# Two-map attention on one core: the value products of a pair of tiles in one run behind the next tile's scores, and three orders that go with it

## The reference, cut to what matters

```python
def diff_attention(q, k, v, pos, slopes, lam):
    # q, k: [B, L, H, 2, 64]; v: [B, L, H, 128]
    def block(qb, pb):
        s = jnp.einsum('bqhmd,bkhmd->bhmqk', qb, k) * scale
        s = s - slopes * dist
        p = jax.nn.softmax(s, axis=-1)
        w = p[:, :, 0] - lam * p[:, :, 1]
        return jnp.einsum('bhqk,bkhe->bqhe', w, v)
```

## Time and profile before

| | |
|---|---|
| median of 3 runs | 3316.82 us (3316.59 to 3317.58) |
| the profiled execution | 3318.04 us, of which span 3316.2 us |
| TensorE matmul busy | 3175.5 us (96%), 19990 instructions |
| TensorE weight loads busy | 2813.7 us (85%) |
| VectorE, ScalarE, GpSimd busy | 54%, 35%, 30% |
| the two-map attention | from about 1306 us of the span to about 1945 us |

### The profile page before, as it was taken

How to read it: one execution, slowest core, us unless ns; L and a number is a source line. 1 busy time by engine, 2 the same in 40 slices (tenths; PEclk the granted TensorE clock), 3 DMA queues, 4 the chain that set the end, 5 groups by cost and what they waited for, 6 DMA issues and landing times.

```text
span 3316.2 us, 51851 instructions
## 1 busy us (share of the span) xinstructions
PE 3175.5 (96%) x19990; PEld 2813.7 (85%) x19990; DVE 1799.1 (54%) x3108; ACT 1145.6 (35%) x2293; POOL 990.4 (30%) x688
## 2 busy tenths in 40 slices
PE   8999999999999999999999889999999999799997
PEld 6677768788888888888888789999999999799997
DVE  5554556755554545788888741277678033522223
ACT  3433333333322213555555541156466110300002
POOL 3112223787772333222221132210000222122222
PEclk9999999999999999999999999999999999899998
DMA  4011112122224112000000012211111341478888
GB/s 158 26 32 33 33 64 102 64 77 77 77 98 195 45 44 97 23 23 23 26 25 22 16 49 85 76 40 51 38 48 45 107 177 56 179 248 311 310 312 291
DMA packets 98390, 315.27 MB, mean 95 GB/s; under 512 B 15266, under 2 KB 31586, under 8 KB 95008
## 3 DMA queue, kind: packets, MB, share of 16 engines
q1 hardware_dynamic: 68448, 248.16, 21.2%
q10 hardware_dynamic: 23600, 45.98, 3.7%
q0 software_dynamic: 6160, 18.63, 2.2%
HBM read 249.55 MB, written 57.86 MB: 93 GB/s over the span
## 4 chain that ended last, share of the span: by engine, by line
PE 45%; DVE 7%; ACT 4%; issue 3%; DMA 1%; POOL 0%; ACTq 0%; SPq 0%; DVEq 0%; POOLq 0%
PE PS L683 14%; PE PS L3733 6%; PE PS L671 4%; PE PS L3480 4%; PE PS L3763 3%; ACT EA L2277 3%; PE PS L3514 3%; PE PS L3272 3%; PE PS L3241 3%; PE PS L3556 3%; PE PS L3316 2%; DVE EA L2754 1%; DVE EA L2738 1%; DVE PA_lo L2765 1%; DVE EB L2916 1%
## 5 line engine op out<-in xcount | busy, mean ns | idle before, releaser
L705 POOL CAST w_hi<-ring 128x1024 fp32r<-128x1024 f32 x130 | 137.8, 1060 | 1568.1 <-PE PS L683 390.4
L707 POOL TENSOR_TENSOR w_lo<-ring,w_hi 128x1024 fp32r<-128x1024 f32 x130 | 326.4, 2511 | 10.5
L2277 ACT ACTIVATE EA<-EA,small_sb 128x1040 f32<-128x1040 f32 x144 | 166.8, 1159 | 222.2 <-DVE small_sb L2738 222.2
L2738 DVE CUSTOM_DVE_ANT_0 EA<-PS,biasH,low_a 128x1024 f32<-128x1024 f32 x128 | 163.6, 1278 | 25.1 <-PE PS L3272 23.1
L3241 PE MATMUL PS<-u_hi,w_hi 128*128 128x348 f32 x504 | 171.1, 339 | 0.5
L3241 PE MATMUL PS<-u_lo,w_hi 128*128 128x348 f32 x504 | 162.2, 322 | 0.0
L3241 PE MATMUL PS<-u_hi,w_lo 128*128 128x348 f32 x504 | 162.0, 321 | 0.0
L1671 DVE TENSOR_TENSOR hid_lo<-hid,hid_hi 128x1024 fp32r<-128x1024 f32 x44 | 91.8, 2124 | 118.7 <-ACT hid_hi L1313 118.7
L1763 PE MATMUL PS<-u_hi,w_hi 128*128 128x512 f32 x352 | 146.9, 417 | 3.0 <-POOL w_lo L707 2.3
L1960 PE MATMUL PS<-t_hi,slot_hi 128*128 128x512 f32 x352 | 139.8, 397 | 5.9 <-DVE t_lo L1572 3.2
L1960 PE MATMUL PS<-t_hi,slot_lo 128*128 128x512 f32 x352 | 139.1, 395 | 0.0
(11 more groups left out here) (522 smaller groups left out, 9017.0 us busy)
## 6 DMA issues: line engine op xcount, KB each, us to landing
ring<-in_stream SPq DMA_DIRECT2D x130, 512.0 KB, 3.5
w_gate_sb<-in_w_gate SPq DMA_DIRECT2D x64, 512.0 KB, 6.9
w_up_sb<-in_w_up SPq DMA_DIRECT2D x64, 512.0 KB, 7.1
w_down_sb<-in_w_down SPq DMA_DIRECT2D x64, 512.0 KB, 5.6
gu_raw<-in_gate_up SPq DMA_DIRECT2D x22, 1024.0 KB, 5.5
hid_keep<-hid_out SPq DMA_DIRECT2D x17, 512.0 KB, 2.9
hid<-hid_keep ACTq DMA_DIRECT2D x15, 512.0 KB, 16.5
x_keep<-xT ACTq DMA_DIRECT2D x1, 4176.0 KB, 14.6
```

The costliest lines, as they stand in the source:

```text
L705: pool.tensor_copy(w_hi[j][:, :, :], w_raw[j][:, :, :]).then_inc(S["w_rounded"], 1)
L707: pool.tensor_tensor(w_lo[j][:, :, :], w_raw[j][:, :, :], w_hi[j][:, :, :], ALU.subtract).then_inc(S["w_split"], 1)
L2277: act.activation(e[0:m, :], e[0:m, :], ACT.Exp, scale=-1.0, bias=small[0:m, 8 + 2 * par + k:9 + 2 * par + k], accum_out=small[0:m, 12 + 2 ...
L2738: dve.tensor_tensor_reduce(e[0:m, 0:T1], wide(2 * k, T1, m), bias, -1.0, low_a[0:m, t, k:k + 1], ALU.add, ALU.min, low).then_inc(S["aa_max ...
```

## The change

`values` is no longer cut into halves. All 27 matmuls of a group stand where the second half stood, behind the scores of the even step; the first half's places at t = 1, 3, 5 and 8 are gone. The two waits for `probs_lo` stay, each ahead of its part. In ScalarE's list `take_columns` moves behind the `exp` of map 1. In the last head's even steps `turn_probs` moves ahead of `woven_gate`. Nothing is computed that was not, and the instructions are the same in number.

```diff
@@ ScalarE, head()
                         if after:
                             exp(after[0], (after[1] + after[2]) % 2, after[2], 0)
-                        if t % 2 == 0 and before:
-                            take_columns(*before)
                         if t % 2 or t == NT:
                             take_pt(h, t)
                         if after:
                             exp(after[0], (after[1] + after[2]) % 2, after[2], 1)
+                        if t % 2 == 0 and before:
+                            take_columns(*before)
                         if t % 2 == 0 and t < NT:
                             take_pt(h, t)
@@ TensorE
-                def values(h, g, half):
+                def values(h, g):
 
                     n, w = 9 * h + A_GROUPS[g][-1], group_width(g)
-                    pe.wait_ge(S["probs_lo"], 3 * n + 2 + half)
-                    if g == 0:
-                        pe.wait_ge(S["values_lo"], 3 * h + 2 + half)
-                    for i in (range(4, NT + 1) if half else range(4)):
+                    for i in range(NT + 1):
+                        if i % 4 == 0 and i < NT:
+                            pe.wait_ge(S["probs_lo"], 3 * n + 2 + i // 4)
+                            if g == 0:
+                                pe.wait_ge(S["values_lo"], 3 * h + 2 + i // 4)
...
-                    if half:
-                        last.then_inc(S["aa_o"], 1)
+                    last.then_inc(S["aa_o"], 1)
@@ TensorE, head()
                         if before:
-                            values(*before, 1)
+                            values(*before)
                         kind, c = UNITS[t]
                         unit(h + 1, 1 - odd, kind, c, 0)
                         turn_probs(h, (odd + t) % 2, t, first)
                         unit(h + 1, 1 - odd, kind, c, 1)
-                        if t in (1, 3, 5, NT):
-                            values(h, min(t // 2, NGA - 1), 0)
                         if before:
                             turn_back(*before, 9 * h + t)
@@ TensorE, the last head
                     if t % 2 == 0:
-                        values(*group_before(h, t), 1)
+                        values(*group_before(h, t))
+                        turn_probs(h, (1 + t) % 2, t, False, False)
                     if t == 0:
                         pe.wait_ge(S["aa_vf"], 3 * h + 3)
                     woven_gate(*WOVEN[t])
-                    turn_probs(h, (1 + t) % 2, t, False, False)
-                    if t in (1, 3, 5):
-                        values(h, t // 2, 0)
-                    if t % 2 == 0:
+                    if t % 2:
+                        turn_probs(h, (1 + t) % 2, t, False, False)
+                    else:
                         turn_back(*group_before(h, t), 9 * h + t)
@@ TensorE, the last head, drain()
-                        for half in range(2):
-                            values(h, NGA - 1, half)
+                        values(h, NGA - 1)
```

## The result

The changed kernel takes 3322.13 us in the median of 13 runs (3318.78 to 3325.03), the kernel before 3316.75 us beside it (13 runs, of which one took 7910 us and doesn't move the median). The ratio is 1.0016, with a 95% interval of 1.0009 to 1.0024: about 5 us slower. That is clear of the noise, but less than the 0.2% that I had called no change. The profiled execution takes 3321.27 us with a span of 3319.5, 3.3 us more than before.

A forecast was written before the change was run, and what follows sets the result against it. TensorE sets the pace of heads 0 to 6, VectorE close behind and pacing the last head. 7 x (0.63 + 0.60 - 1.31) + 6 x 0.35 - 0.3 = +1.3 us, so 3318 us, no change; range 3298 to 3325.

The forecast's parts named there:

- rival (a): Steps 3 and 6: columns not late, VectorE has slack; gains 1.09 and 1.31 us a head, 3299 us; chance 0.13.
- the pairs of steps: Steady heads: steps 1 and 2 take 17.2 us (before 16.58), 3 and 4 18.3 (17.70), 5 and 6 17.7 (19.01).
- T1: Start of step 1 on TensorE; VectorE's first pass over step 2's scores was put 9.84 us after it.
- T3: Start of step 3 on TensorE; VectorE's first pass over step 4's scores was put 10.94 us after it.
- Step 4's wait: Steady heads, step 4: transposes wait 1.7 us for the columns; steps 3 and 4 together +0.60 us a head.
- The wait of step 8: Step 8: not removed, 1.5 us at meta_scores; 1.60 us of products move into step 0; +0.35 us in heads 1 to 6.
- In step 6: Step 6: no wait ahead of turn_back; steps 5 and 6 together -1.31 us a head (bound -0.9).
- Rival (b): Step 3: VectorE's short copy slips ahead of GpSimd's L707; 1.15 us less in step 4, 3310 us; chance 0.14.
- +0.27: Steady heads: a head of 80.4 us against 80.17.
- rival (c): Heads: clock falls behind step 4's wait of 1.7 us; 12 us over 7 heads, 3330 us; chance 0.08.
- -0.3 us: Last head: -0.43 in steps 1, 3, 5; +0.1 in steps 2, 4; +0.8 in step 6; step 0 even.
- S + 4.16: TensorE's transposes can start 4.16 us after S, the start of VectorE's first pass over that step's scores.

The follow-up runs named there:

- V: Kernel before, only all value products of a group put behind the next tile's scores: 3306.18 us, ratio 0.9962.
- C: Kernel before, only take_columns put behind the second exponential: 3327.7 us, ratio 1.0032.
- G: Kernel before, only the last head's even steps turning tiles ahead of the gate's products: 3314.12 us, ratio 0.9994.
- the reduction: VectorE's 16-column copy of meta_a issued as a reduction over a length-1 axis: 3296.64 us in the changed kernel, 3299.14 us in the kernel before.

## Why the prediction was right, and where it wasn't

**Right, by its steps.** The sum of a gain and a loss near each other was the answer: V takes the waits ahead of the values away, C puts waits ahead of the transposes. What I had as rival (a), that the columns are not late, 3299 us, is what the kernel without C does (3300.6). The lengths of the pairs of steps came within 0.13 us of the forecast, each a little shorter, since I started VectorE's pass some 0.1 to 0.2 us late (it comes at T1 + 9.63 in step 2, forecast 9.84, and at T3 + 10.72 in step 4, forecast 10.94). Step 4's wait is 1.47 us instead of 1.7. The wait of step 8 stood up at the meta scores, as the order had shown. In step 6 there is none. Rival (b) stayed close: in step 3 the copy starts 0.09 us behind L707, where it was 0.23:

```profile
1572.78 2.40 POOL L707 TENSOR_TENSOR w_lo<-ring,w_hi 128x1024 fp32r<-128x1024 f32 x1
1572.87 2.34 DVE L2735 COPY EA<-meta_a 128x16 f32<-128x16 f32 x1
```

From step 1 of head 0 to step 1 of the last I had +1.5 us, and measured +1.9, but that they are so close is luck. The steps themselves didn't lengthen a head (80.2 us where the clock stays up, 80.1 to 80.5 before), where I had +0.27 for most. Three falls of the clock, 0.95 each, added 2.9 us that I hadn't priced, and head 0, head 2 and head 6 came out 0.3, 0.3 and 0.7 us shorter than before. Of the 5 us by which the kernel is slower, the forecast had 1.3.

**Wrong: the clock in the heads.** I priced a fall in step 4, behind the wait of 1.7 us, as rival (c), 0.08 and 12 us. It came in step 0 instead, behind the wait of 1.46 us at the meta scores, and in three heads alone. A wait of the same length at the same clock stood before in step 8 without a fall, with 12 value products behind it; the experiment that puts them back has no falls, and over all the traces the half clock follows the wait at the meta scores 13 times of 36, and the one ahead of value products never. I moved these products and kept the wait, but didn't ask what the clock would make of that.

**Wrong: the last head.** I had -0.3 us, from -0.43 for each odd step and little for the even ones. Steps 1 to 7 became 0.7 longer. The pairs of steps take 16.88, 16.95 and 17.65 us instead of 17.52, 17.27 and 15.96, where I expected about 17.2, 16.9 and 16.3. The first two fit by luck: before, they held one fall of the clock each, in the scores of steps 1 and 3, which I left in and which is gone; in its place the transposes of steps 2 and 4 run at half clock. The last pair had no fall before, and there the new one shows: in step 6 I had a gate piece of 12 matmuls, but not the half clock that it now runs at. That TensorE would stand 3.4 us in one piece followed from my own numbers (transposes at S + 4.16), and half a clock behind such a stretch was in sight in the earlier trace rows; I wrote that the clock could be worth 3 us either way and put nothing in the sum. That G makes this worse the text said in words (the gate "now stands behind it"), but priced at some tenths: by the ratios it is 4 to 6 us. Step 2 is 1.7 us longer than in the changed kernel without G (12.40 against 10.70). From its transposes to `turn_back` it has 3.63 us; the same work at full clock takes 2.41 in step 2 of the kernel with G alone, its wait taken off, and without G there are 1.90 us, a wait of 0.76 in them. So by this estimate the order is worth 0.5 us a step, near my tenths, and the half clock 1.2.

**Not foreseen: the tail.** From step 7 to the output projection takes 1.4 us more. Windows of about 9 us from the first transposes of the finished heads, the kernel before and then the changed one:

```profile
1954.00:1963.00 9.00, 6.66 (x37) 6.42 (x38) 4.29 (x6) 2.23 (x2) 3.81 (x3) 0.81 0.42 163
1963.00:1972.00 9.00, 9.00 (x70) 8.93 (x69) 4.71 (x5) 4.47 (x4) 8.48 (x6) 1.00 0.12 30
```

```profile
1956.00:1965.00 9.00, 5.49 (x38) 5.21 (x39) 4.50 (x5) 2.24 (x2) 4.25 (x3) 0.97 0.40 156
1965.00:1974.00 9.00, 9.00 (x59) 8.95 (x58) 4.16 (x4) 3.45 (x4) 6.97 (x5) 0.84 0.17 48
```

The clock is low once in each, for about the same time. Before, it is low ahead of a wait for `oa_lo`, which hides it; after, the wait comes first (3.52 us instead of 2.13) and the low clock falls on 59 matmuls, where there were 70. All kernels with any of the three parts have some of it, 1.3 to 3.3 us; the two with none (the kernel before, and it with the reduction) have 43.8 to 43.9 us there. What sets it I can't say.

**Open.** The medians differ by 5.4 us and the two traces by 3.3. The time up to the first head's step 1 also varies by up to 6 us between the profiles (1307.1 to 1313.0), though next to nothing was changed there. So a share of some us in any one account is not explained. Each kernel has one trace only, and the mean granted clock of the kernel before lies between 0.979 and 0.984 over its executions, so the falls need not be the same in each. Why L2705 gets in ahead of L707 in some heads and not in others was not tried either.

## What to carry to other kernels

When a change bundles several moves, price each alone and then in pairs: here one gained 13 us, one lost 11, and the third seems to change sign with the second, while the whole measured as nearly nothing. A wait that only moves still counts, since what stands behind it decides whether it is followed by dense work or by the next wait. And before an order is tuned around a late engine, look at the longest of its short instructions: that one and the same copy took 0.17 us or 2.4 was worth 19 us on the kernel before and 26 on the changed one, more than the best of the moves' combinations (17).

## What the runs showed of the hardware

A copy of 16 columns lasts 0.17 us, or 1.85 to 2.38 in the heads' steps 3 and 8 where GpSimd's L707 is under way; a start of 0.09 us behind L707 is enough. As a reduction it lasts at most 0.172 in all 144 cases. A subtraction with both operands in SBUF is held in the same way (2.70 us instead of 0.50), and L707 itself takes 3.24 to 3.27 us instead of 2.40 where it starts within L2754, and some 3.7 where L2705 gets in ahead of it as well.

TensorE's clock fell from 2.4 to 1.2 GHz (granted 1.00 and 0.50) in some heads and not in others of one execution, though they do the same work: behind the wait of 1.40 to 1.46 us ahead of the meta scores in three of six. Where 12 value products stand between such a wait and the scores it didn't fall once in 41 cases; where they don't, 13 times in 36. Behind waits of 3.4 us in the last head the transposes ran at half clock in all three even steps of the changed kernel. With the reduction in, after the same waits (3.33 to 3.39 us), they took 1.14 us, and in two of the three the next scores 1.01 and 1.05 instead of 0.73. So the length of the wait doesn't tell by itself where the fall comes.
